# A decoder layer step on one core: the entry chain reordered, with projections begun on 8 of 16 feature tiles and the forget gate in four column groups

## The reference

```python
h = layer_norm(x, ln_emb_g, ln_emb_b)                  # prompt and sample rows
z = h @ w_in                                           # (.., 2048) x (2048, 11272)
rq, rk, rv, rg, fq, fk, fv, ff, gr, gf = split(z)      # ff: 8 columns, one per forgetting head
logf = log_sigmoid(ff + b_f)
...                                                    # retention, forgetting attention
c = cumsum(concat([logf_past, logf_new]))              # logf_past from cache pages
mix = (sigmoid(gr) * y_r + sigmoid(gf) * y_f) @ w_out
x1 = layer_norm(ALPHA * h + mix, ln1_g, ln1_b)
y = layer_norm(ALPHA * x1 + (silu(x1 @ w1) * (x1 @ w3)) @ w2 + sigmoid(x1 @ w_pg) * (p @ w_pe), ln2_g, ln2_b)
```

## Time and profile before

| | us |
|---|---|
| median of 3 runs | 1928.5 |
| lowest and highest | 1928.49 and 1933.37 |
| the profiled execution's own time | 1936.93 |
| its span | 1935.4 |
| PE busy | 1849.2 |
| DVE busy | 1050.0 |
| ACT busy | 793.8 |
| POOL busy | 148.6 |

### The profile page before, as it was taken

One profiled execution on the slowest core, in us unless ns is written; L12 is line 12 of the kernel. 1 busy time (PEld: TensorE's weight loads), 2 busy tenths in 40 slices (PEclk: granted clock), 3 DMA queues, 4 the chain that ended last, 5 costly groups with the idle time before them and its releaser, 6 DMA issues.

```text
span 1935.4 us, 39410 instructions
## 1 busy us (share of the span) xinstructions
PE 1849.2 (96%) x14346; PEld 1743.8 (90%) x14346; DVE 1050.0 (54%) x2097; ACT 793.8 (41%) x930; POOL 148.6 (8%) x262
## 2 busy tenths in 40 slices
PE   5999999999899999999988999999999999999996
PEld 4999998888777877889978999999999999999995
DVE  5444575764767667447656554444444444444554
ACT  2453424434434433324335445555433344443333
POOL 3340101111121112000000000000000000000000
PEclk9999999999999999899998999999999999999998
DMA  5555677787899899545533555665555665655551
GB/s 158 145 158 161 210 247 227 245 282 236 256 336 316 303 343 317 173 153 184 180 119 126 174 185 177 184 185 182 178 179 180 186 181 180 183 176 174 180 179 45
DMA packets 318258, 386.18 MB, mean 200 GB/s; under 512 B 16377, under 2 KB 293369, under 8 KB 317785
## 3 DMA queue, kind: packets, MB, share of 16 engines
q1 hardware_dynamic: 286832, 287.48, 47.9%
q0 software_dynamic: 28352, 95.84, 14.3%
q10 hardware_dynamic: 2992, 1.79, 0.4%
HBM read 371.21 MB, written 13.84 MB: 199 GB/s over the span
## 4 chain that ended last, share of the span: by engine, by line
PE 72%; DVE 4%; DMA 2%; issue 2%; ACT 1%; POOLq 0%; DVEq 0%; ACTq 0%; SPq 0%
PE acc L509 22%; PE acc L510 22%; PE acc L514 22%; PE X L634 2%; DMA page<-in_cache_v 2%; PE X L759 1%; PE X L822 1%; DVE pagesum L1252 1%; DMA raw<-in_w_in 1%; PE X L623 1%; PE X L644 0%; DVE uT L1500 0%; DVE wlo L452 0%; PE X L616 0%; ACT whi L447 0%
## 5 line engine op out<-in xcount | busy, mean ns | idle before, releaser
L452 DVE TENSOR_TENSOR wlo<-raw,whi 128x1024 fp32r<-128x1024 f32 (+1 forms) x552 | 659.0, 1202 | 653.0 <-ACT whi L447 646.1
L447 ACT ACTIVATE whi<-raw 128x1024 fp32r<-128x1024 f32 (+1 forms) x552 | 568.8, 1037 | 678.9 <-PE acc L514 668.8
L509 PE MATMUL acc<-x_hi,whi 128*128 128x264 f32 x1664 | 413.9, 286 | 10.7 <-DVE x_lo L1509 6.8
L510 PE MATMUL acc<-x_lo,whi 128*128 128x264 f32 x1664 | 413.3, 285 | 0.0
L509 PE MATMUL acc<-hT_hi,whi 128*128 128x264 f32 x1408 | 365.4, 296 | 0.0
L510 PE MATMUL acc<-hT_lo,whi 128*128 128x264 f32 x1408 | 355.1, 288 | 0.0
L509 PEld LDWEIGHTS acc<-x_hi,whi 128*128 128x128 f32 x1664 | 314.2, 189 | 11.9 <-issue 7.4
L510 PEld LDWEIGHTS acc<-x_lo,whi 128*128 128x128 f32 x1664 | 315.7, 190 | 0.0
L509 PEld LDWEIGHTS acc<-hT_hi,whi 128*128 128x128 f32 x1408 | 270.4, 192 | 41.7 <-issue 38.3
L510 PEld LDWEIGHTS acc<-hT_lo,whi 128*128 128x128 f32 x1408 | 271.7, 193 | 0.1
L514 PE MATMUL acc<-x_hi,wlo 128*128 128x264 f32 x1664 | 236.6, 285 | 0.0
(11 more groups left out here) (300 smaller groups left out, 1722.9 us busy)
## 6 DMA issues: line engine op xcount, KB each, us to landing
raw<-in_w SPq DMA_DIRECT2D x256, 512.0 KB, 4.0
raw<-in_w_in SPq DMA_DIRECT2D x176, 512.0 KB, 4.8
page<-in_cache_k POOLq DMA_DIRECT2D x64, 512.0 KB, 6.3
page<-in_cache_v POOLq DMA_DIRECT2D x64, 512.0 KB, 5.6
raw<-in_w_out SPq DMA_DIRECT2D x32, 512.0 KB, 4.4
raw<-in_w_pg SPq DMA_DIRECT2D x32, 512.0 KB, 3.5
stateS<-in_state_ret POOLq DMA_DIRECT2D x8, 1024.0 KB, 8.2
out_ret_state_sample<-stateS POOLq DMA_DIRECT2D x8, 1024.0 KB, 7.3
```

The source lines that it names most:

```text
L447: nc.scalar.activation(whi[:, s, 0:k, :], raw[:, s, 0:k, :], ACT.Copy).then_inc(S["hi_made"], 1)
L452: nc.vector.tensor_tensor(wlo[:, s, 0:k, :], raw[:, s, 0:k, :], whi[:, s, 0:k, :].bitcast(F32), ALU.subtract).then_inc(S["lo_made"], 1)
L509: mm(backward(acc[c.acc][:, m, 0:T]), w, backward(xh[:, c.kt0 + t, :]), start=c.first and t == 0, stop=False)
L510: mm(backward(acc[c.acc][:, m, 0:T]), w, backward(xl[:, c.kt0 + t, :]), start=False, stop=False)
```

## The change

- SP loads the sample rows first. DVE takes the statistics of the sample rows and of rows 0 to 127, ACT makes their square roots, and ACT now normalises rows 0 to 127 while DVE takes the statistics of rows 128 to 255 and then normalises the sample rows and those. The bias and scale of ACT's step are those of the other half.
- PE transposes 8 tiles, runs chunk 0, transposes 4 tiles, runs chunk 1, transposes 4 tiles, and goes on with chunk 2.
- The forget gate is one product after chunk 3: `wff` is padded with zeros to 32 columns and becomes the stationary operand, and `h32` moves with all its 264 columns. Tile k goes to column group k mod 4, so that four partial sums stand in partitions 0, 32, 64 and 96 of a bank. DVE copies them (`ffp`), and after chunk 4 three small matmuls with a constant `pick` (128 by 8, four identities stacked) add the four groups and turn the result round. `p` is transposed after chunk 5. The steps of DVE and ACT behind them move into the loop over chunks too.
- ACT splits chunks 0 and 1 before its first `hT_hi`, and chunk 2 behind the eighth.
- POOL clears `wff`, waits for the prompt, and issues the five loads that ACT's queue had issued, `wff` first, all ahead of its first `hT_lo`.
- `Lc` and `ffp` lie at other places of the page buffers.

The diff, cut to its core:

```diff
+        "pick": np.tile(np.eye(32)[:, 0:8], (4, 1))
-        wff = place("wff", [P, DT, H_F], F32, at=after("h32"))
+        wff = place("wff", [P, DT, 32], F32, at=after("h32"))
-        Lc = place("Lc", [P, DEC * NPG, H_F], F32, at=made["page"][0])
+        Lc = place("Lc", [P, DEC * NPG, H_F], F32, at=made["page"][0] + 4096)
+        ffp = place("ffp", [P, T], F32, at=made["page"][0] + 8192)
@@ sync
+            sp.dma_start(xtok[0:DEC, 2, :], a["x_sample"]).then_inc(x_in[2], 16)
             for t in range(2):
                 sp.dma_start(xtok[:, t, :], a["x_prompt"][t * P:(t + 1) * P]).then_inc(x_in[t], 16)
-            sp.dma_start(xtok[0:DEC, 2, :], a["x_sample"]).then_inc(x_in[2], 16)
@@ tensor
-            pe.wait_ge(S["wff_in"], 16)
-            pe.wait_ge(S["h_made"], DT)
-            for t, (lo, n) in enumerate(((0, P), (P, P), (SEQ, DEC))):
+            def forget_partial():
+                pe.wait_ge(S["wff_in"], 16)
+                pe.wait_ge(S["h_made"], DT)
                 for k in range(DT):
-                    last = mm(X[0:n, 0, t * 8:t * 8 + 8], h32[:, k, lo:lo + n], wff[:, k, :], start=k == 0, stop=k == DT - 1)
-            last.then_inc(S["ff_ps"], 1)
+                    g = k % 4 * 32
+                    last = mm(X[g:g + 32, 0, 0:T], wff[:, k, :], h32[:, k, :], start=k < 4, stop=k >= DT - 4)
+                last.then_inc(S["ff_part_ps"], 1)
+            def forget_rows():
+                pe.wait_ge(S["ff_part_sb"], 1)
+                for t, (lo, n) in enumerate(((0, P), (P, P), (SEQ, DEC))):
+                    last = mm(X[0:n, 1, t * 8:t * 8 + 8], ffp[:, lo:lo + n], const("pick"), start=True, stop=True)
+                last.then_inc(S["ff_ps"], 1)
...
+            stream_T(0, 8)
             for it in range(phF.iters):
                 for j in range(len(phF.chunks)):
                     multiply(phF, it, j)
+                    if it == 0 and j < 2:
+                        stream_T(8 + j * 4, 12 + j * 4)
+                    if it == 0 and j == 3:
+                        forget_partial()
+                    if it == 0 and j == 4:
+                        forget_rows()
+                    if it == 0 and j == 5:
+                        entry_T()
@@ scalar
-            act.wait_ge(x_in[1], 16)
-            act.dma_start(cst[:, n_first:n_const], ...)
-            act.dma_start(wff[:, :, :], ...)
-            act.dma_start(bf[:, :], ...)
-            act.dma_start(ptok[:, 0:2, :], ...)
-            act.dma_start(ptok[0:DEC, 2, :], ...)
...
+            A(xtok[:, 0, :], xtok[:, 0, :], ACT.Identity, bias=stat[:, 48:49], scale=stat[:, 44:45]).then_inc(S["xn_act_made"], 1)
+            act.wait_ge(S["ln_var"], 3)
+            A(stat[:, 41:42], stat[:, 35:36], ACT.Sqrt, bias=eps_ln).then_inc(S["ln_std"], 1)
+            for j in range(2):
+                split_hi(act, phF, 0, j)
             for k in range(DT):
                 act.wait_ge(S["h_made"], k + 1)
                 A(hT_hi[:, k, :], h32[:, k, :], ACT.Copy).then_inc(S["h_hi"], 1)
+                if k == 7:
+                    split_hi(act, phF, 0, 2)
@@ vector
+            row_stats(2, DEC)
+            row_stats(0, P)
...
+            row_stats(1, P)
...
+                if k == 3 or k == 7:
+                    split_lo(dve, phF, 0, k // 4)
+            split_lo(dve, phF, 0, 2)
...
                     split_lo(dve, phF, it, j + AHEAD)
+                    if it == 0 and j == 4:
+                        forget_partial()
+                    if it == 0 and j == 5:
+                        forget_size()
+                    if it == 0 and j == 7:
+                        forget_log()
@@ gpsimd
+            nc.gpsimd.memset(wff[:, :, :], 0.0).then_inc(S["wff_zero"], 1)
+            pool.wait_ge(S["wff_zero"], 1)
+            pool.wait_ge(x_in[1], 16)
+            pool.dma_start(wff[:, :, 0:H_F], ...)
+            pool.dma_start(cst[:, n_first:n_const], ...)
+            pool.dma_start(bf[:, :], ...)
+            pool.dma_start(ptok[:, 0:2, :], ...)
+            pool.dma_start(ptok[0:DEC, 2, :], ...)
             for k in range(DT):
                 pool.wait_ge(S["h_hi"], k + 1)
```

More of the change, by code:

```diff
@@ L92, in shape_constants @@
     parts = {
-        "ident": np.eye(P), "eps": np.tile([[1e-5, 1e-6]], (P, 1)), "le": le, "ones": ones, "gt": gt,
+        "ident": np.eye(P), "pick": np.tile(np.eye(32)[:, 0:8], (4, 1)), "eps": np.tile([[1e-5, 1e-6]], (P, 1)), "le": le, "ones": ones, "gt": gt,
         "mask": np.concatenate([causal, np.zeros((P, P)), causal], 1),
@@ L387, in r_slot @@
             return "middle" if n else "first", (None, n)
+        n_first = where["eps"][0] + 2
         block = ctx.enter_context(nc.Block())
@@ L471, in _ @@
             pe.wait_ge(S["xn_act_made"], 1)
[L472 to L480, removed]
@@ L494, in _, with stream_T @@
-            last.then_inc(S["pT_ps"], 1)
+            def stream_T(k0, k1):
+                for k in range(k0, k1):
+                    b = k % 4
+                    if k == 0:
+                        pe.wait_ge(S["cst_par"], 2)
+                    if k >= 4:
+                        pe.wait_ge(S["h_made"], k - 3)
+                    for t in range(2):
+                        tr(X[:, b, t * P:(t + 1) * P], xtok[:, t, k * P:(k + 1) * P], ident)
+                    tr(X[:, b, SEQ:T], xtok[0:DEC, 2, k * P:(k + 1) * P], ident[0:DEC, 0:DEC]).then_inc(S["xT_ps"], 1)
@@ L495, in backward, with entry_T @@
+            def entry_T():
+                pe.wait_ge(S["p_in"], 32)
+                for k in range(2):
+                    for t in range(2):
+                        tr(X[:, 2 + k, t * P:(t + 1) * P], ptok[:, t, k * P:(k + 1) * P], ident)
+                    last = tr(X[:, 2 + k, SEQ:T], ptok[0:DEC, 2, k * P:(k + 1) * P], ident[0:DEC, 0:DEC])
+                last.then_inc(S["pT_ps"], 1)
             def backward(ap):
@@ L858, in _ @@
             act.dma_start(prow[96:104, :], a["gn_g"].rearrange("(r c) -> r c", c=P)).then_inc(S["parrows_in"], 16)
[L859 to L864 removed]
             act.wait_ge(S["ident_in"], 16)
[L867 removed]
             eps_ln, eps_gn = const("eps")[:, 0:1], const("eps")[:, 1:2]
[L869 removed]
+            for t, n in ((2, DEC), (0, P)):
+                act.wait_ge(S["ln_var"], 1 if t == 2 else 2)
                 last = A(stat[0:n, 40 + t:41 + t], stat[0:n, 32 + 2 * t + 1:32 + 2 * t + 2], ACT.Sqrt, bias=eps_ln[0:n, :])
@@ L876, in _, with forget_log, entry_hi @@
                 A(hT_hi[:, k, :], h32[:, k, :], ACT.Copy).then_inc(S["h_hi"], 1)
-                if k % 6 == 5 and k // 6 < 1:
-                    split_hi(act, phF, 0, 0)
-            for j in range(1, AHEAD):
-                split_hi(act, phF, 0, j)
-            act.wait_ge(S["cst_in"], 16)
-            act.wait_ge(S["lsg_abs"], 1)
-            link.step(A(stat[:, 0:16], stat[:, 0:16], ACT.Exp, scale=-1.0))
-            link.step(A(small[0:8, 3, 0:8], small[0:8, 3, 0:8], ACT.Exp, scale=-1.0))
-            A(stat[:, 0:16], stat[:, 0:16], ACT.Ln, bias=1.0)
-            A(small[0:8, 3, 0:8], small[0:8, 3, 0:8], ACT.Ln, bias=1.0).then_inc(S["lsg_ln"], 1)
-            act.wait_ge(S["pT_ps"], 1)
-            A(pT_hi[:, :, :], X[:, 1:3, 0:T], ACT.Copy).then_inc(S["p_hi"], 1)
+                if k == 7:
+                    split_hi(act, phF, 0, 2)
+            def forget_log():
+                act.wait_ge(S["lsg_abs"], 1)
+                link.step(A(stat[:, 0:16], stat[:, 0:16], ACT.Exp, scale=-1.0))
+                link.step(A(small[0:8, 3, 0:8], small[0:8, 3, 0:8], ACT.Exp, scale=-1.0))
+                A(stat[:, 0:16], stat[:, 0:16], ACT.Ln, bias=1.0)
+                A(small[0:8, 3, 0:8], small[0:8, 3, 0:8], ACT.Ln, bias=1.0).then_inc(S["lsg_ln"], 1)
+            def entry_hi():
+                act.wait_ge(S["pT_ps"], 1)
+                A(pT_hi[:, :, :], X[:, 2:4, 0:T], ACT.Copy).then_inc(S["p_hi"], 1)
             def fox_values(it):
@@ L1162, in _ @@
                     .then_inc(S["h_made"], 1)
-            for j in range(AHEAD):
-                split_lo(dve, phF, 0, j)
-            dve.wait_ge(S["h_lo"], DT)
-            dve.wait_ge(S["ff_ps"], 1)
-            dve.wait_ge(S["bf_in"], 16)
-            zt, zs = stat[:, 16:32], small[0:8, 3, 8:16]
-            V.tensor_tensor(zt.rearrange("p (t h) -> p t h", t=2), X[:, 0, 0:16].rearrange("p (t h) -> p t h", t=2),
-                            bf[:, :].unsqueeze(1).broadcast_to([P, 2, H_F]), ALU.add)
```

78 lines of the change are left out of this document (45 added, 33 removed).

## The result

| | before | changed |
|---|---|---|
| median of 5 runs, us | 1930.88 | 1918.84 |
| lowest and highest, us | 1928.49 to 1939.50 | 1917.19 to 1923.19 |
| the profiled execution's own time, us | 1936.93 | 1920.96 |
| its span, us | 1935.4 | 1919.4 |

The ratio is 0.9936, with a 95% interval of 0.9921 to 0.9952: 12 us less, clear of noise. The time, 1918.84, lies inside the forecast range of 1907 to 1921 and 5.3 us above the forecast 1913.5: 3 us are gain that did not come, and 2.4 us are the base, since two more runs of the kernel before moved its median from 1928.5 to 1930.88.

The account below looks back on a forecast made before the run. PE, busy 1849.2 of 1935.4 us, was taken as the bound. Chunk 6 starts 19.2 us earlier; the page wait leaves 16.6, the clock behind it 15, so 1928.5 becomes 1913.5, range 1907 to 1921.

Parts of the forecast that it names:

- First transpose: Entry: PE's first transpose of a feature tile at about 17.3 us, ends 16.3 and 18.5, against 22.60 before.
- Chunk 0: Entry: eight transposed tiles and POOL's four low parts both ready at 23.9 us, against a start at 52.75 before.
- The clock: Interleaved stage: chunk 0 still costs 5.3 us and raises the pace; later chunks take 2.9 us.
- The rival with the clock low through the stage: Entry: chunks 1 and 2 stay at 5.3 us, transposes at 3.3; gain 11 us, time 1917.5; chance 0.23.
- The sixteenth low part: POOL, entry: last transpose at 36.7 us, the last low part 2.7 later at 39.4, against 38.5 before.
- The gate: After chunk 3: sixteen products take 3.5 us, half of 7.1 in a row; ends 1.8 and 7.1.
- What is given back: Ahead of `past_bias`: PE arrives at 139.5 us, pages at 142.1, a new wait of 2.6; gain 16.6 instead of 19.2.
- The clock after the wait: Behind the page wait: a slower clock costs up to 2.5 us or nothing; about half, 1.3, taken off 16.6.
- POOL as the bound: POOL, entry: the five load issues take over 26 us instead of 4 and all gain is lost; chance 0.04.
- the serial gate: After chunk 3: column groups run one by one, 7.1 us; PE 15.6 earlier, no wait, 1913; no separate chance given.
- a failed early start: Entry: late sample rows or slow DVE-ACT steps, and a low clock; gain about 5 us, 1923.5; chance 0.06.
- The rival with the full 19.2 us: Page loop not in the way, or a clock dip elsewhere goes; PE's whole gain comes through, 1909; chance 0.14.

Follow-up runs that it names:

- second set: The unaltered change run again beside the kernel before on one chip: median 1920.46 us against 1930.35, ratio 0.9951.
- d4: e1 with the five later loads issued by ACT again, ahead of its square roots, instead of POOL: 1921.90 us, ratio to before 0.9937.
- d5: The kernel before with only the five loads moved from ACT's queue to POOL's: 1928.62 us, ratio to before 0.9985.
- f1: e1 with DVE's low part of chunk 2 computed right behind that of chunk 1: 1914.17 us, ratio to before 0.9906.
- e1: The changed kernel with the page table's load issued as POOL's first instruction: 1908.67 us, ratio to before 0.9897; run again 1913.03 us, 0.9904.
- e3: The changed kernel with `past_bias` and its evacuation behind chunk 10 of the second pass instead of chunk 6: 1912.02 us, ratio to before 0.9918.
- e2: The kernel before with only the page table's load moved to be POOL's first instruction: 1930.95 us, ratio to before 1.0001.
- d1: e1 with all 16 tiles transposed ahead of chunk 0 again: 1913.31 us, ratio to before 0.9897.
- d2: e1 with the gate in its old form of 48 products, at the new place behind chunk 3: 1922.90 us, ratio to before 0.9934.

## Why the prediction was right

The direction, the mechanism and the range held: PE gains about 22 us in the entry, POOL's page loop does not move with it, and a new wait ahead of `past_bias` takes part of it back. The size came out at 12 us (9 on the second set) where 15 was forecast. At the start of `past_bias` PE was 16.95 us earlier (158.68 against 141.73), with 16.6 forecast; that this agrees so closely is partly luck, as the points on the page loop show. Point by point:

- **First transpose**, 17.3 forecast, 16.01 measured. The sample rows landed at 3.94, near the lower bound of 3.5, and not at 5.5. d4 and d5 bear out the step that needs both edits.
- **Chunk 0**, 23.9 forecast, 22.54 measured. The loads of chunks 0 and 1 had landed by 15.67, not 19, probably because the constants now came later and over another queue (not tested). I had taken unchanged. The two chains nearly tied all the same, not through the loads but through the tiles: POOL's fourth low part was done at 22.06.
- **POOL's five loads**, 4 us and hidden: 4.3 us and hidden.
- **The clock**, up after chunk 0: right, and chunk 1 took 3.0. The rival with the clock low through the stage does not occur in any of the traces; 2 us of transposes between chunks did not undo it. Chunk 0 itself took 4.1 where 5.3 was forecast, and 4.1 to 5.5 in the other traces.
- **The sixteenth low part**, 39.4 forecast, 38.2 measured: the transposes ended 3 us earlier than forecast (33.7 against 36.7), but the last low part came 4.5 us behind them instead of 2.7, because POOL's last four took 4.8 us. The earlier trace rows mixes both paces: fifteen of the 16 low parts took 0.75 us each, and the last, with DVE's subtractions beside it, 1.6. f1 shows what makes the difference.
- **The gate**, 3.5 forecast, 1.92 measured. Four column groups did overlap nearly four times: 7.1/1.92 = 3.7, where 7.1 is the estimate for sixteen in a row, which no run shows. The rule of the Trainium skill (TensorEngine Tiling (Array Packing), Theoretical Speedup), up to four times, gave an estimate of 1.8 and was nearer than the row with two groups. As forecast, this only lengthened the wait.
- **What is given back.** The page loop was forecast to release PE at 142.1, and did at 141.7. Two errors cancel in this: the last low part ended 1.2 us earlier than forecast, and from there to the first page it took 6.4 us instead of 5.2 (5.2 again in the second trace, where the release came at 141.1). The wait was 4.54 instead of 2.6, because PE was there 2.3 us earlier than forecast, at 137.2. e1, e3 and e2 show this mechanism from three sides.
- **The clock after the wait** is the term that was mis-sized: 1.3 us taken, half of the 2.5 of one chunk; measured 3.1 and 1.8 in the two traces of the change. What stands behind this wait is not a chunk of 2.9 us but the 4.13 us of `past_bias`, and the clock stayed low over most of it: its first product doubled (1.02 to 2.04 us), the others took 5.38 us instead of 3.25.
- **The rest**: 13.8 us ahead at 149 us in one trace, 15.8 in the other, and 9 to 12 us at the end by medians. The profiled execution of the kernel before lay 6 us above its median, so its span (16.0 longer than the changed kernel's) overstates the gain. The traces can say whether something is lost behind `past_bias`. From the chunk behind it to the end, the three traces with the old entry (before, e2, d5) take 1772.6, 1764.1 and 1767.5 us, on average 1768.1. The eight with the new entry and `past_bias` in its place (the change twice, e1 twice, d1, d2, d4, f1) take 1761.9 to 1774.1, on average 1769.1. The averages differ by 1 us where single executions differ by 12. So no loss is shown there, though one of a few us is not excluded, and the 2 to 6 us that are missing lie within the spread.

POOL as the bound, the serial gate and a failed early start did not happen. The rival with the full 19.2 us describes e1, not the change.

## What to carry to other kernels

When the engine that sets the end is moved forward by 20 us, everything that it later consumes has to be dated again: a chain with 17 us to spare on an engine that does not move with it becomes the new wait, and one instruction moved there was worth another 5.5 to 7.7 us by the traces, beside the 9 to 12 of the change itself (e1 against the change). A part of a change is priced on a base where nothing else binds; with the page wait in place, its slack of 4.5 us would have hidden part of each of them. The price on such a base is not the price in the change, though: the interleaving is worth 0.7 us there, while in the change it also holds back the page loop. Reordering two engines that wait on each other can be a loss with either half alone (24.5 and 20.2 against 22.6) and the gain with both (16.0).

## What the runs showed of the hardware that was not expected

- A stream of float32 products with 128 weight columns and only 8 moving columns ran at a granted clock of 0.87 over its first 3.25 us and of 0.50 from there on, though PE was counted busy throughout (d2, one trace). The chunk behind it took 4.75 us instead of 2.9.
- The same wait of 2.9 us stands in twelve traces, and the chunk behind it took from 3.0 to 5.4 us, 1.2 us more on average than without the wait. One look at the clock after a short wait decides nothing; the average over many traces does.
- POOL's subtraction took 0.72 us without DVE's subtractions of SBUF operands beside it and 1.2 with them, where their work overlapped, and DVE's subtraction took 1.5 us instead of 1.2; a single such overlap cost PE a microsecond (e1, f1).
- The load of one short row copied to 128 partitions held ACT's queue for 5.0 us (before and d4) and POOL's for 0.54 (after).
- In the entry the records give a granted clock of 1.00 while the pace is that of 1.2 GHz (chunk 0 before): there the pace of like instructions has to be read, not the column.
